# Four small reorderings in a two-block transformer kernel: the chunk loop's r-k product, one bank read, the group norm's squares, and norm factors spread by transposes

## The reference

```python
# first block
h = rms_norm(x, norm_mix_pre); proj = h @ w_in
attn = sliding_window_sink_attention(q, k, v, rel_bias, sinks)      # 8 heads, window 128
p = p + (p_prev - p) * rwkv_shift_mix                               # token shift
# rwkv7 time mix, 8 heads of 64 channels, r, k, v, decay, kk, a per token:
state = state * w_t + sa * (kk_t * a_t) + v_t * k_t ;  o_t = state @ r_t
o = group_norm(o) * ln_x_g + ln_x_b
o = o + sum(rh * kh * r_k) * vh                                     # bonus
x = x + rms_norm(concat(attn, o * g) @ w_out, norm_mix_post)
f = conv_gated_ffn(rms_norm(x, norm_ffn_pre), ...)
x = x + rms_norm(f, norm_ffn_post)
# second block
h = rms_norm_2(x) * (1 + scale) + shift ; p = h @ w_in_2
o_a, o_b = gated linear attention (chunks), o_c = stick-breaking attention
x = x + gate * (concat(o_a, o_b, o_c) @ w_out_2)
return rms_norm_2(x) * final_norm_w
```

## Time and profile before

| | |
|---|---|
| median of three runs | 2710.59 us (2708.94 to 2710.78) |
| profiled execution, its own time | 2721.02 us |
| its span | 2718.1 us |
| PE busy | 94% |
| DVE busy | 44% |
| ACT busy | 25% |
| POOL busy | 32% |
| mean granted PE clock | 0.955 |

### The profile page before, as it was taken

One profiled execution on the slowest core, in us unless ns is written; L12 is line 12 of the kernel. 1 busy time (PEld: TensorE's weight loads), 2 busy tenths in 40 slices (PEclk: granted clock), 3 DMA queues, 4 the chain that ended last, 5 costly groups with the idle time before them and its releaser, 6 DMA issues.

```text
span 2718.1 us, 45342 instructions
## 1 busy us (share of the span) xinstructions
PE 2547.7 (94%) x18310; PEld 2039.4 (75%) x18310; DVE 1197.2 (44%) x1577; ACT 688.0 (25%) x1035; POOL 874.4 (32%) x498
## 2 busy tenths in 40 slices
PE   8999889988969999999999999999979999988887
PEld 6777589975867888888888888877868777733576
DVE  4477766644465331332133213325360666634252
ACT  3233433321122210221022002212332322255521
POOL 3332000011303443344334433465654455400021
PEclk9999999988959999999999999999989999989798
DMA  4211000002521111111111111133311111220021
GB/s 146 66 32 34 26 3 4 4 18 112 174 85 39 46 47 54 46 46 46 54 46 46 46 53 47 46 135 106 124 62 47 44 48 50 74 78 1 1 90 65
DMA packets 44351, 155.97 MB, mean 57 GB/s; under 512 B 4264, under 2 KB 6568, under 8 KB 43688
## 3 DMA queue, kind: packets, MB, share of 16 engines
q1 hardware_dynamic: 26784, 97.53, 11.1%
q10 hardware_dynamic: 17416, 56.31, 5.8%
HBM read 133.37 MB, written 20.45 MB: 57 GB/s over the span
## 4 chain that ended last, share of the span: by engine, by line
PE 81%; DVE 10%; ACT 4%; issue 2%; DMA 1%; POOL 1%; DVEq 0%; ACTq 0%; POOLq 0%
PE ps L493 50%; PE ps L1021 5%; PE ps L599 5%; PE ps L1044 2%; DVE proj L114 2%; ACT ab L114 2%; PE ps L1121 1%; DVE x_lo L114 1%; PE ps L548 1%; PE ps L773 1%; PE ps L770 1%; PE ps L763 1%; DMA ada_w<-wada 1%; DVE nrm_a L114 1%; DVE xx L114 1%
## 5 line engine op out<-in xcount | busy, mean ns | idle before, releaser
L398 POOL TENSOR_TENSOR w_hi<-w_raw,small 128x1024 fp32r<-128x1024 f32 x178 | 339.9, 1910 | 1529.3 <-PE ps L493 1165.1
L493 PE MATMUL ps<-x_hi,w_hi 128*128 128x512 f32 x1600 | 512.3, 394 | 36.4 <-DVE x_lo L114 17.3
L493 PE MATMUL ps<-x_lo,w_hi 128*128 128x512 f32 x1600 | 508.2, 392 | 0.0
L493 PE MATMUL ps<-x_hi,w_lo 128*128 128x512 f32 x1600 | 507.8, 391 | 0.0
L401 POOL TENSOR_TENSOR w_lo<-w_raw,w_hi 128x1024 fp32r<-128x1024 f32 x178 | 440.2, 2473 | 14.0
L493 PEld LDWEIGHTS ps<-x_hi,w_hi 128*128 128x128 f32 x1600 | 301.2, 189 | 106.7 <-issue 18.9
L493 PEld LDWEIGHTS ps<-x_hi,w_lo 128*128 128x128 f32 x1600 | 302.5, 189 | 63.5
L493 PEld LDWEIGHTS ps<-x_lo,w_hi 128*128 128x128 f32 x1600 | 302.7, 189 | 62.9
L114 DVE SCALAR_TENSOR_TENSOR cv<-ps,cst,cv 128x1023 f32<-128x1023 f32 x64 | 82.1, 1282 | 258.1 <-ACT cv L114 252.7
L493 PE MATMUL ps<-f_hi,w_hi 128*128 128x512 f32 x512 | 170.8, 394 | 3.8 <-POOL w_lo L401 3.8
L493 PE MATMUL ps<-f_lo,w_hi 128*128 128x512 f32 x512 | 169.2, 391 | 0.0
(11 more groups left out here) (289 smaller groups left out, 3857.6 us busy)
## 6 DMA issues: line engine op xcount, KB each, us to landing
w_raw<-wall SPq DMA_DIRECT2D x178, 512.0 KB, 3.5
ada_w<-wada ACTq DMA_DIRECT2D x24, 512.0 KB, 4.9
fill_spill<-stage ACTq DMA_DIRECT2D x24, 256.0 KB, 2.0
x_in<-xT ACTq DMA_DIRECT2D x8, 512.0 KB, 8.6
x<-xT ACTq DMA_DIRECT2D x1, 4096.0 KB, 12.8
x_spill<-x ACTq DMA_DIRECT2D x1, 4096.0 KB, 11.0
x_in<-x_spill ACTq DMA_DIRECT2D x2, 2048.0 KB, 12.8
x_spill<-x ACTq DMA_DIRECT2D x2, 2048.0 KB, 8.3
```

What stands on the lines that cost most here:

```text
L398: nc.gpsimd.tensor_tensor(w_hi[:, u, :, :], w_raw[:, u, :, :], sm["one"].unsqueeze(2).to_broadcast([P, KT, P]), ALU.mult).then_inc(S("w_hi ...
L493: last = mm(ps[:, 2 * u + h, :], w[:, u, k, :], x[:, k, h * 512:(h + 1) * 512], start=(k == 0 and w is w_hi and x is hi), stop=(k == KT - ...
```

## The change

Four edits. The first makes the same number of calls with another instruction, the others only move operations:

1. `half_spread` and `norm_sum` spread the norm factors by `nc.tensor.transpose` of the broadcast column, where a matmul with the identity stood.
2. ACT copies each attention tile to `x_hi` behind the square of the centered tile of the same number, where all four copies stood ahead of the squares; DVE makes the `x_lo` tiles between and behind the copies of the centered tiles, where all four stood ahead.
3. DVE's `taken(1)` stands between `logits(0, 0)` and `logits(0, 1)`, and `shift(1)` behind `weights(0, 1)`, where both stood inside the first slot of the loop.
4. `receptance_keys(n + 3)` stands at the end of the round in the chunk loop, behind `level_in(n, 4)`.

```diff
-                    last = mm(half_bank(lane, i)[:, t * P:(t + 1) * P], sm[f"inv_{lane}"][:, t:t + 1].to_broadcast([P, P]),
-                              par("ident"), start=True, stop=True)
+                    last = turned(half_bank(lane, i)[:, t * P:(t + 1) * P],
+                                  sm[f"inv_{lane}"][:, t:t + 1].to_broadcast([P, P]), par("ident"))
...
-                    last = mm(rs_of(n)[:, t * P:(t + 1) * P], sm["nri"][:, t:t + 1].to_broadcast([P, P]), par("ident"),
-                              start=True, stop=True)
+                    last = turned(rs_of(n)[:, t * P:(t + 1) * P], sm["nri"][:, t:t + 1].to_broadcast([P, P]), par("ident"))
...
-            for k in range(4):
-                copy(x_hi[:, k, :], mix_src[k]).then_inc(S("x_hi_done"), 1)
             for m in range(4):
                 act.wait_ge(S("cen_mm"), m + 1)
                 if m >= 2:
                     act.wait_ge(S("gn_mm"), m - 1)
                 fn(osq[:, m % 2, :], pair(2 * (m % 2)), ACT.Square).then_inc(S("gn_sq"), 1)
+                copy(x_hi[:, m, :], mix_src[m]).then_inc(S("x_hi_done"), 1)
...
             logits(0, 0)
+            taken(1)
             logits(0, 1)
-            filled, fresh = 1, True
+            filled, fresh = 2, False
...
                         if b == 0:
                             weights(0, 0)
-                        weights(b, 1)
+                            weights(0, 1)
+                            shift(1)
+                        else:
+                            weights(b, 1)
...
                     prepare_b(n + 3)
-                    receptance_keys(n + 3)
...
                 if late(n):
                     level_in(n, 4)
+                if 0 <= n + 3 < N_CHUNK:
+                    receptance_keys(n + 3)
...
-            for k in range(4):
-                low(1, k, mix_src[k])
             for m in range(4):
                 dve.wait_ge(S("gn_sq"), m + 1)
                 vcopy(o1[:, m, :], pair(2 * (m % 2))).then_inc(S("oc_done"), 1)
+                if m:
+                    low(1, m - 1, mix_src[m - 1])
+            low(1, 3, mix_src[3])
```

More of the change, by code:

```diff
@@ L479, in _ @@
             mm = nc.tensor.matmul
+            turned = nc.tensor.transpose
             def gemm(g, u, hi, lo, first=False, parts=None, hs=(0, 1), k0=0, k1=KT):
```

## The result

| | kernel before | change |
|---|---|---|
| time, us: median (lowest to highest, runs) | 2710.62 (2708.94 to 2710.78, 4) | 2684.88 (2682.95 to 2686.95, 4) |
| ratio to before, 95% interval | | 0.9907 [0.9889, 0.9924] |
| profiled execution, us; its span | 2721.02; 2718.1 | 2682.95; 2681.2 |
| mean granted TensorE clock | 0.955 | 0.962 |

The account below looks back on a forecast made before the run. TensorE (PE), busy 94% of the span, was taken to bound the kernel. The terms 3.5 + 6.5 + 14.9 + 7.2 = 32.1 us took the median from 2710.6 to 2678.5 us, range 2672 to 2692.

Parts of the forecast that it names:

- Part 1: Attention start: earlier bank read by DVE shortens PE's wait and half 3 starts earlier; 3.5 us, range 0 to 3.8.
- Part 2: Chunk loop: r-k product behind the last masked copy takes 0.50 off 13 PE waits; 6.5 us, range 4 to 7.
- Part 3: Group norm behind the loop: reordered squares and x_hi/x_lo copies bring the variance read 14.9 us earlier, range 10 to 17.
- Part 4: Norm factor spreads: transposes need half the records of identity products, saving 5.4 plus 1.8, together 7.2 us.
- A: Attention start and group norm both stay at PE's lower clock: total gain 22, giving 2689 us; chance 0.12.
- B: Group norm: GpSimd holds DVE so each x_lo takes 2.4 us; 4.6 less gain, 2683 us; chance 0.08.
- C: Norm spreads: a transposed call takes a quarter of a product's time; 10.7 instead of 7.2, 2675 us; chance 0.04.
- D: Weight stream or x reload behind the group norm sets the time, gain given back: within 5 us of 2710; chance 0.03.
- E: Chunk loop loses the upper clock, a chunk growing by up to 14 us, so the kernel is slower; chance 0.03.

Follow-up runs that it names:

- e7: Kernel before with only DVE's half of the group norm edit (x_lo between the copies, ScalarE's order as before): 2713.16 us against 2714.3, ratio 1.0001.
- e8: The change with x_lo 2 and 3 behind the variance read and shift(1) behind taken(2), against the kernel before: 2686.34 us against 2714.3, ratio 0.9903.
- r_after: The change run once more, unaltered, against the kernel before: 2687.74 us against 2714.3, ratio 0.9901.
- e5: Kernel before with one more DVE product per new chunk ahead of m2 in the chunk loop: 2723.99 us, ratio 1.0049 to the kernel before.
- e9: Kernel before with only ScalarE's half of the group norm edit (first two squares ahead of the four x_hi copies): 2716.72 us, ratio 1.0011.
- e4: Kernel before with only the norm factors spread by transposes: 2704.22 us against 2714.87, ratio 0.9965.
- e3: Kernel before with only the group norm edit (squares first, x_hi and x_lo behind): 2701.49 us against 2714.87, ratio 0.9953.
- e2: Kernel before with only the r-k product (receptance_keys) moved behind the last masked copy in the chunk loop: 2709.86 us against 2714.87, ratio 0.9982.
- r_before: Kernel before run once more, unaltered: 2716.09 us against 2710.70 of the other runs of the same code, ratio 1.0011.

## Why the prediction was right, and where its size was off

**Part 1, forecast 3.5.** The order of events came as worked out: a wait of 1.80 ahead of the scores (about 1.9), half 3 at 112.98 (113.3), the clock at 1.00 from 103 to 112 us. What failed is the other side of the difference. The 8.59 us of half 2 at the lower clock was taken for a property of the kernel before; it is nearly the longest of eight (5.7 to 8.6), so half 3 moved by 3.9 in the profiled pair, by 2.5 against the executions at 115.5 and by 1.0 against e7. What survives to the loop's start: 346.6 on average over the eight executions with the old attention start, 344.2 over the five with the new one (e8 left out), 2.4 us. Alone it measured 2.7 by its ratio. The term was mis-sized by about 1; since equal code starts the loop 3.4 us apart (after and r_after), that figure is itself uncertain by as much.

**Part 2, forecast 6.5.** 6.4 on average (239.6 to 233.2), and the six executions with the moved product lie within 0.2 us of each other. The chunk period is 14.15 in the trace after (456.05 to 470.20 between two m2 products), forecast 14.1. The queue of PE would have let it start at 447.47 (448.01 less the idle of 0.54) and not at 447.3 as the prediction has it; the gain of 0.50 stands either way. The step that mattered was reading which DVE operation is last before PE's wait, and that nothing in the loop reads the moved product; e5 confirms it from the other side.

**Part 3, forecast 14.9.** The variance read moved by 14.8, and both waits named were needed: DVE's half alone gives 3 us at the variance and none that the times show (e7), ScalarE's alone turns 3.85 of waiting into 9.07 elsewhere (e9). With the early clock return of e4 the same edit would have given 8.4. To the gate it is 38.3 (the mean of five executions with the old order) against 23.3 (after, r_after and e3): 15.1; with e4 among the old ones 14.0.

The choice to leave the first spread at the lower clock was right (3.28 to 3.68 for its 32 records, 1.97 would be the upper). The rule cited there was about who wins between x_lo 0 and the split: GpSimd had started first (582.48 against 583.00), so the variance was not 0.6 better.

**Part 4, forecast 7.2.** Locally 7.2. From the gate to the end, however, it is 2088.9 on average over the eight executions without transposes and 2082.8 over the six with them: 6.1. Two of the eight, before and e2, lie at 2091; against the other six it is 5.3. Part of what is missing is in the price: at 3.78 us each spread was read off one execution, and in r_before the three take 3.54, 3.78 and 3.64. Stretch by stretch, the spreads' own sections shrank by 1.6 to 2.4 us each, and the section from the turning products (2036.3 in r_before, 2003.0 in after) to the last spread grew from 660.3 to 662.2 (it is 660.1 to 660.3 in six executions without transposes and 662.2 in all six with them; before and e2 have 663.6 and 663.7). One window of it, 80 us from the same point, r_before and after, the columns as above:

```profile
2354.00:2434.00 80.00, 71.96 (x288) 38.52 (x286) 34.16 (x80) 33.97 (x57) 10.02 (x6) 0.91 0.28 105
```
```profile
2321.00:2401.00 80.00, 73.91 (x286) 39.21 (x284) 33.03 (x77) 32.38 (x56) 10.02 (x6) 0.87 0.28 105
```

About as many matmuls, but PE's clock is 0.87 in place of 0.91, and PE is busy 2 us longer for them. The window cut in the same way shows 0.87 in all six executions with transposes and 0.91 in all eight without, so this goes with the change. It is not the whole account, since before and e2 have 0.91 too and the longest section. What in the shorter spreads ahead of it lowers the clock was not tried, and stays open.

**The sum, and the step that failed.** From the table: 2.4 + 6.4 + 14.0 to 15.1 + 6.1 make 29 to 30, against 32.1. The mean span of before, r_before and e9, whose edit gave nothing, is 2715.8, of after and r_after 2684.1: 31.7; that few traces can't tell 29 from 32. The medians say 25.7 and, in the second measurement, about 27, with intervals that reach to 30 and 31. So some 2 to 3 of the missing 6.4 us are the terms of parts 1 and 4. The rest has no place in the traces; it is no more than the intervals allow, and the 32.1 itself lies just outside both.

The step behind it is the one in the prediction's second paragraph: "The sum below is made against the profiled one, and the difference is taken off the median." The profiled execution lies 10.4 above the median and at the lower end of the granted clock, as the long ones of the 73 runs do. Against the mean of the eight traces with the old attention start its loop starts 2.0 us late, and its end lies 2.3 us further behind the gate than the mean without transposes. The first of these is the stretch in which part 1 is priced. A gain that is read off there cannot be taken in full from a median that doesn't hold all of that cost. Part 3, the largest term, was not made too large in this way: its 31.4 stands in five executions of six. So this step explains about 1 us by measurement, and that it explains more of the gap is argued and not shown. The prediction had the means to see it: the 10.4 us had no explanation in it.

**The rivals.** A (the clock stays low in both stretches) is refuted: 1.84 us for 16 records of the sums, 1.00 through half 2. B (every x_lo held) too: one is held (2.91), the others take 1.23 and 1.27. C (a quarter) too, with 24 records of 427 ns where 48 were: the rule of the Trainium skill, "TensorE: Matmul & The Clock Gate", section "Terms", that was weighed in part 4 (four times faster for f32) does not show here; the measured factor is two. D (given back) is refuted by the end of the span, and E (the loop loses the clock) by the granted clock between 345 and 560 us, 0.99 in after and 0.98 before.

## What to carry to other kernels

Take a gain from one trace against another execution's median only after asking what made the profiled execution longer: if it is a stretch at the lower clock and the edit lies in it, price the edit once with that stretch at the upper clock as well, and carry both. Where two engines each hold a third one up, moving one of them may give little or nothing (3 us of 15 in e7, none in e9); look for the next wait before judging half a change. And a wait of half a microsecond in every round of a loop is worth more certainty than a single one of four: in the traces the first came out within 0.1 us of the forecast, and the second missed it by about 1.

## What the runs showed of the hardware

- The same instructions behind the same PE wait (3.66 us) took from 8.62 down to 5.71 us in eight executions of seven programs that are alike up to there: when the upper clock returns after an idle is not fixed by the instructions ahead. Behind the wait of 3.85 in the group norm it was back within 10 us once (e4: 592.70 to 602.58), and in r_before not in 24 us of work (595.04 to 618.8) with one more wait of 2.97 among them.
- A transpose of an f32 column broadcast to 128 by 128 is one record of the length that each of a product's two has, at either clock (427 against 431 ns, 272 against 274).
- Four x_lo operations took 9.71 us beside GpSimd's splits (r_before) and 7.15 when they began some 3 us later (e9); alone, one takes 1.23. A DVE operation that is held ends about as late as GpSimd's plus its own run: 2.91 us from 583.00 for one that takes 1.23, with the split ending at 584.83. GpSimd is held in its turn: the two splits beside the x_lo of r_before took 2.88 and 3.22 us, where 1.89 and 2.35 is their time in the change.
- Equal code, timed twice on one chip, read 2710.7 and 2716.1 as medians of 23 and 12 runs. Over 73 runs of it the time goes with the mean granted clock: below 2709 us with 0.958 to 0.960, above 2715 us with 0.955 to 0.957.
